# Joining the two products with the high weight into one 512-column matmul (second layer's gate/up)

## Chip, cores, metric

One core of one Trainium2 chip. The metric is the device time of one execution in microseconds, as the median of several runs. The kernel before takes 1451.1 us (three runs, 1447.51 to 1451.57).

## What is computed

Two transformer blocks on 256 tokens of width 1024, one after the other. The second one has two layers, and in its second layer only the 256 latent tokens go on (the context is no longer needed), so its SwiGLU works on 256 columns:

```python
def swiglu(h, w_gate_up, w_down):
    gu = h @ w_gate_up
    g, u = jnp.split(gu, 2, axis=-1)
    return (jax.nn.silu(g) * u) @ w_down
...
h = h + g_f * swiglu(modulate(rmsnorm_2(h, norm_ffn[i]), sh_f, sc_f), ffn_w_gate_up[i], ffn_w_down[i])
```

`w_gate_up` is 1024 x 5632 in float32 (2816 features of gate, as many of up). The stage that computes `gu` and `silu(g) * u` in the second layer is called `gu1` in the kernel; `dn1` is the product with `w_down` after it.

## The kernel before

**Numbers in two parts.** TensorE multiplies in fp32r. Weights and activations are each split into a high part (a cast) and a low part (the rest): x = xh + xl, w = wh + wl. A product is three matmuls into the same PSUM place: wh with xh, wh with xl, wl with xh (`three`, lines 1050 to 1054). The weights are the stationary operand, 128x128; the activations, features on partitions and tokens on columns, the moving one: 256 columns in `gu1`, 512 in the first layer's `gu0`.

**Weights.** They come from memory in units of 128x1024 (four k tiles by 256 features, 512 KB), into four slots. For each unit SyncE starts the transfer into `raw` (line 392), ScalarE casts `raw` to `wh` (`high`, line 637), GpSimd subtracts to make `wl` (`low`, line 547), and TensorE waits for that (`unit_ready`). ScalarE casts a unit only when TensorE is done with the unit four before it. A step is two units: all 8 k tiles for 256 features.

**The stage.** In gate/up the 256 features of a step are 128 of gate and the 128 of up that belong to them: a pair. There are 22 steps, unrolled by two in a loop; the first trip is written out. For one output tile (gate or up) TensorE runs over four k tiles of a unit, three matmuls each. Gate and up of 256 columns each share one bank: pair j of the two uses bank j (`tile_bank`, `pair_banks`). Pairs alternate, so TensorE fills one while the other is read.

After a pair is done, `gate_up` of ScalarE (line 859) and of VectorE (line 1668) work on it in turn: Silu of the gate half (line 867), product with the up half (line 1674, which frees the pair), the high part of f (ScalarE, line 870), its low part (VectorE, line 1677). The order on ScalarE is by hand. A trip for pair j is: the casts of the two units of the next step (`high_step`), then Silu and high part for pair j. So the casts for step j+2 stand behind Silu and high part of pair j.

**Around it.** Ahead of the stage the activations are normalized and split (lines 1488 to 1496 and 741); behind it comes `dn1`, for which `stream_summed` first loads another activation table (line 665) and then goes on with the casts. The names that the change adds are `xhl` (xh and xl in one tile), `sf` (a place in SBUF for the copied halves), `joined` and the semaphores `small_gu1` and `joined_gu1`.

Of the kernel before, what the change touches and what calls it, by code (L numbers as in the profile page):

```python
# [8 lines left out]
F32R = mybir.dt.float32r  # L9
BF16 = mybir.dt.bfloat16  # L10
ALU = mybir.AluOpType
ACT = mybir.ActivationFunctionType
AX_X = mybir.AxisListType.X

P = 128
D = 1024
KT = D // P
SEQ = 256
NT = 2 * SEQ
# [86 lines left out]
ADA_SLOTS = 4  # L106
ADA_WOVEN = {"out": (3, 3, 0, 6)}
OUT_ROWS = ((0, 1, 2), (3,), (4,), (5,))
IN_U = (0, 1, 4, 5, 2, 3, 6, 7)
_at = 6  # L110
for _n, _per, _slots in (("gu", 1, 2), ("dn", 3, 3), ("gu0", 2, 2), ("dn0", 3, 2)):
# [35 lines left out]
def build(nc, wall, wada, cond, xin, pin, par, tab, tab_ret, tab_rope, tab_mask, rpb, out):  # L147
    with ExitStack() as ctx:
        sems = {}

        def S(name):
            if name not in sems:
                sems[name] = ctx.enter_context(nc.semaphore(name))
            return sems[name]
# [8 lines left out]
        def at(name, shape, offset, dt=F32):  # L163
            size = 4 * int(np.prod(shape[1:]))
            assert offset + size <= base + arena_bytes, (name, offset + size - base - arena_bytes)
            return nc.alloc_sbuf_tensor_at(name, shape, dt, offset=offset)

        def sb(name, shape, dt=F32):
            o = cursor[0]
            cursor[0] = (o + 4 * int(np.prod(shape[1:])) + 31) // 32 * 32  # L170
            return at(name, shape, o, dt)

        class Region:
# [5 lines left out]
            def take(self, name, shape, dt=F32):  # L179
# [5 lines left out]

        h = sb("h", [P, KT, NT])
        xs_at = cursor[0]
        xh = sb("xh", [P, KT, NT], F32R)
        xl = sb("xl", [P, KT, NT], F32R)
        y = sb("y", [P, KT, NT])  # L190
        y_at = cursor[0] - 4 * KT * NT
        raw = sb("raw", [P, SLOTS, HALF, 256])
        wh = sb("wh", [P, SLOTS, HALF, 256], F32R)
        wl = sb("wl", [P, SLOTS, HALF, 256], F32R)
# [18 lines left out]
        fh = {SEQ: at("fh1", [P, FT, SEQ], big_at, F32R), NT: at("fh2", [P, FT, NT], big_at, F32R)}  # L213
        fl = {SEQ: at("fl1", [P, FT, SEQ], big_at + 4 * FT * SEQ, F32R),
              NT: at("fl2", [P, FT, NT], big_at + 4 * FT * NT, F32R)}
        sil = at("sil", [P, 2, NT], y_at)
        ft = at("ft", [P, 2, NT], y_at + 8 * NT)

# [57 lines left out]
        ps = ctx.enter_context(nc.psum_tensor("ps", [P, 8, 512], F32))  # L276
# [6 lines left out]
        bank_free = S("bank_free")  # L283
# [5 lines left out]
        def pair_banks(j, n, wide=False):  # L289

            if n == SEQ and wide:
                return ps[:, 2 * j:2 * j + 2, 0:SEQ]
            if n == SEQ:
                return ps[:, j, :].rearrange("p (a b) -> p a b", a=2)
            return ps[:, 2 * j:2 * j + 2, :]

        def tile_bank(j, o, n, wide=False):

            return ps[:, j, o * SEQ:o * SEQ + SEQ] if n == SEQ and not wide else ps[:, 2 * j + o, 0:n]
# [29 lines left out]
        def pair_done(eng, ph, i, pair):  # L329

            eng.wait_ge(units_done, i * (2 * ph.body) + (2 * ph.step0 + 2 * ph.per_pair * (pair + 1) + SLOTS))
# [57 lines left out]
        def _(sp):  # L389
# [86 lines left out]
            sp.dma_start(ident[:], tab).then_inc(S("tab_in"), 16)  # L476
            load(0, 0, IN_U[0])
            sp.dma_start(prm[:], par).then_inc(S("prm_in"), 16)
            for u_ in range(1, SLOTS):
                load(u_, u_, IN_U[u_])  # L480
            for u_ in range(SLOTS, SLOTS + 2):
                load(u_, u_ % SLOTS, IN_U[u_])
            sp.dma_start(csb[:], bass.AP(cond.tensor, 0, [[0, P], [D, 2], [1, D]])).then_inc(S("cond_in"), 16)
# [148 lines left out]
        def _(act):  # L632
# [226 lines left out]
            def gate_up(ph, n, f0):  # L859

                def body(i, ahead=0):
                    for j in range(2):
                        if j >= ahead:
                            high_step(ph, i, j)
                        pair_done(act, ph, i, j)
                        act.wait_ge(S("f_lo"), i * 2 + (f0 + j + 1))
                        nc.scalar.activation(sil[:, j, 0:n], tile_bank(j, 0, n), ACT.Silu).then_inc(S("silu_ready"), 1)  # L867
                        act.wait_ge(bank_free, i * 2 + (ph.pair0 + j + 3))
                        settled(act)
                        nc.scalar.activation(fh[n][:, i * 2 + j, :], ft[:, j, 0:n], ACT.Copy).then_inc(S("f_hi"), 1)  # L870
                if ph.name == "gu1":
                    second_step(ph)
                if ph.name != "gu0":
                    preload(ACT.Silu)
                body(0, 1)
                with act.Fori(1, ph.iters) as i:
                    body(i)
# [6 lines left out]
            ph = PH["pg"]  # L884
# [15 lines left out]
            for l in range(2):  # L900
# [124 lines left out]
                n = NT if l == 0 else SEQ  # L1025
# [14 lines left out]
        def _(pe):  # L1040
# [9 lines left out]
            def three(o, wa, wb, xa, xb, start, stop):  # L1050

                nc.tensor.matmul(o, wa, xa, start=start, stop=False, skip_group_check=True)  # L1052
                nc.tensor.matmul(o, wa, xb, start=False, stop=False, skip_group_check=True)  # L1053
                return nc.tensor.matmul(o, wb, xa, start=False, stop=stop, skip_group_check=True)  # L1054

            def features(ph, n, a=xh, b=xl, ktiles=KT, fresh=None, wide=False, within=None):


                def body(i):
                    for j in range(ph.body):  # L1060
                        pair = j // ph.per_pair
                        if j % ph.per_pair == 0:
                            banks_ready(ph, i, pair)
                        for half in range(2):
                            slot = unit_ready(ph, i, j, half)
                            k0 = 2 * HALF * (j % ph.per_pair) + HALF * half
                            for o in range(2):
                                c = slice(o * P, o * P + P)
                                if within and isinstance(i, int) and (i, j) == (0, 0) and (half, o) in within:
                                    within[half, o]()  # L1070
                                for kk in range(min(HALF, ktiles - k0)):
                                    k = k0 + kk
                                    if fresh and o == 0 and pair == 0:
                                        sem, n0, each = fresh
                                        pe.wait_ge(S(sem), n0 + each * (k + 1))
                                    mm = three(tile_bank(pair, o, n, wide), wh[:, slot, kk, c], wl[:, slot, kk, c],
                                               a[:, k, 0:n], b[:, k, 0:n], k == 0 and (n == NT or wide or o == 0), k == ktiles - 1)
                            mm.then_inc(units_done, 1)
                run(pe, ph, body, ph.iters - 1 if within else 0)
# [108 lines left out]
            for c in range(CONV_T):  # L1188
                mm = nc.tensor.matmul(ps[:, 2, 0:SEQ], ones[:], cy[:, c, :], start=c == 0, stop=c == CONV_T - 1)
# [13 lines left out]
            for hd in range(RET_H):  # L1203
                pe.wait_ge(S("ret_s"), hd + 1)
                c = slice(hd * P, hd * P + P)
                nc.tensor.matmul(ps[:, 6, c], st[:, hd, 0:P], vb[:, 0, c], start=True, stop=True)
                nc.tensor.matmul(ps[:, 7, c], st[:, hd, P:256], vb[:, 0, c], start=True, stop=False)
                mm = nc.tensor.matmul(ps[:, 7, c], st[:, hd, 256:384], vb[:, 1, c], start=False, stop=True)
            mm.then_inc(S("ret_o"), 1)
            pe.wait_ge(S("dev_sq"), 1)  # L1210
            for c in range(CONV_T):
                mm = nc.tensor.matmul(ps[:, 5, 0:SEQ], ones[:], sq[:, c, 0:SEQ], start=c == 0, stop=c == CONV_T - 1)
# [3 lines left out]
            for hd in range(RET_H):  # L1216
                for t in range(2):
                    mm = nc.tensor.transpose(ps[:, hd // 2, (hd % 2) * 256 + t * P:(hd % 2) * 256 + t * P + P],
                                             on[:, t, hd, :], ident[:])
# [35 lines left out]
            for l in range(2):  # L1255
                n = NT if l == 0 else SEQ
# [188 lines left out]
        def _(dve):  # L1445
            link = Link(dve, "dve_link")
            V = nc.vector
# [171 lines left out]
            def take_summed(ph, dst, norm):  # L1619

                for p in range(4):
                    if ph.name == "out":
                        condition(ph, 0, 0, OUT_ROWS[p])
                    else:
# [43 lines left out]
            def gate_up(ph, n, f0):  # L1668
                def body(i):
                    for j in range(2):  # L1670
                        condition(ph, i, j)
                        dve.wait_ge(S("f_lo"), i * 2 + (f0 + j + 1))
                        dve.wait_ge(S("silu_ready"), i * 2 + (f0 + j + 1))
                        V.tensor_tensor(ft[:, j, 0:n], sil[:, j, 0:n], tile_bank(j, 1, n), ALU.mult).then_inc(bank_free, 1)  # L1674
                        dve.wait_ge(S("f_hi"), i * 2 + (f0 + j + 1))
                        f1 = bass.ds(i * 2 + j, 1)
                        V.tensor_tensor(fl[n][:, f1, :].rearrange("p a b -> p (a b)"), ft[:, j, 0:n],  # L1677
                                        fh[n][:, f1, :].rearrange("p a b -> p (a b)").bitcast(F32),
                                        ALU.subtract).then_inc(S("f_lo"), 1)
                run(dve, ph, body)  # L1680
# [12 lines left out]
            ph = PH["in_u"]  # L1693
# [121 lines left out]
            for l in range(2):  # L1815
                n = NT if l == 0 else SEQ
# [292 lines left out]
```

## Time and profile before

| | |
|---|---|
| median of three runs | 1451.1 us |
| profiled execution | 1450.42 us, span 1448.6 us |
| granted TensorE clock, mean | 0.981 |
| TensorE busy | 1403.9 us (97%) |
| GpSimd busy | 841.1 us (58%) |
| VectorE busy | 710.3 us (49%) |
| ScalarE busy | 607.0 us (42%) |
| the stage `gu1` | from about 1247 to 1374.9 us |
| the stage `dn1` | 1374.9 us to about 1439 us |

Times in the trace are from the start of the span. The table's busy shares are over the whole span; the stage of the change is about 9% of it and has to be read by itself. Matmuls overlap one another, so that the duration of one (0.28 us for 256 columns) is not its cost; the distance from one start to the next is.

### The profile page before, as it was taken

How to read it: one execution, taken by the hardware profiler on the slowest of the kernel's cores; microseconds unless marked ns; L12 is line 12 of the kernel's file. 1: busy time of each engine (PE TensorE's matmuls, PEld its weight loads, DVE VectorE, ACT ScalarE, POOL GpSimd, SP SyncE). 2: the span in 40 equal slices, each digit the busy share in tenths (PEclk: the TensorE clock that was granted, in tenths of full speed). 3: DMA queues.
4: the chain of work that ended last, by engine and by line, in shares of the span. 5: the costliest groups of instructions: out<-in, count | busy, mean ns of one | idle time of the engine just before them, and what ended most of it. 6: DMA issues, size and time to landing. Idle time of an engine off the chain costs nothing.

```text
span 1448.6 us, 25731 instructions
## 1 busy us (share of the span) xinstructions
PE 1403.9 (97%) x9145; PEld 1256.8 (87%) x9145; DVE 710.3 (49%) x1324; ACT 607.0 (42%) x973; POOL 841.1 (58%) x420
## 2 busy tenths in 40 slices
PE   9998999999999999799999999999999999999998
PEld 8988999999888888687888888888888788999997
DVE  5977555555714555836655555333424383311111
ACT  5454554544524445634332332322331365444452
POOL 5836788797474676052444344544365443588895
PEclk9998999999999999899999999999999999999999
DMA  7836477785332222031656555554393102455563
GB/s 255 267 112 211 160 275 274 276 309 171 123 102 73 74 73 88 1 117 61 228 176 210 184 185 207 185 179 141 86 255 99 44 18 68 132 180 184 177 211 105
DMA packets 82987, 227.27 MB, mean 157 GB/s; under 512 B 23664, under 2 KB 29040, under 8 KB 82672
## 3 DMA queue, kind: packets, MB, share of 16 engines
q1 hardware_dynamic: 82480, 224.91, 46.7%
q10 hardware_dynamic: 448, 1.57, 0.5%
q8 instruction: 37, 0.61, 0.2%
q14 instruction: 22, 0.18, 0.0%
HBM read 222.26 MB, written 1.05 MB: 154 GB/s over the span
## 4 chain that ended last, share of the span: by engine, by line
issue 37%; PE 30%; POOL 27%; DVE 3%; ACT 2%; POOLq 1%; DMA 0%; ACTq 0%; DVEq 0%
POOL wl L547 25%; PE ps L1052 6%; PE ps L1054 6%; PE ps L1053 6%; PE ps L1139 1%; PE ps L1115 1%; PE ps L1116 1%; PE ps L1117 1%; PE ps L1386 1%; PE ps L1125 1%; POOL xl L567 1%; PE ps L1312 1%; PE ps L1333 1%; PE ps L1400 1%; PE ps L1378 1%
## 5 line engine op out<-in xcount | busy, mean ns | idle before, releaser
L547 POOL TENSOR_TENSOR wl<-raw,wh 128x1024 fp32r<-128x1024 f32 x310 | 743.3, 2418 | 542.4 <-ACT wh L637 542.0
L1052 PE MATMUL ps<-xh,wh 128*128 128x256 f32 (+1 forms) x1728 | 562.3, 325 | 10.7 <-DVE y L1629 4.3
L1053 PE MATMUL ps<-xl,wh 128*128 128x256 f32 (+1 forms) x1728 | 556.6, 322 | 0.0
L1054 PE MATMUL ps<-xh,wl 128*128 128x256 f32 (+1 forms) x1728 | 556.3, 322 | 0.0
L637 ACT ACTIVATE wh<-raw 128x1024 fp32r<-128x1024 f32 x310 | 318.7, 1053 | 285.8 <-PE ps L1054 205.0
L1052 PEld LDWEIGHTS ps<-xh,wh 128*128 128x128 f32 x1728 | 332.1, 192 | 43.0 <-issue 8.2
L1054 PEld LDWEIGHTS ps<-xh,wl 128*128 128x128 f32 x1728 | 331.8, 192 | 24.3
L1053 PEld LDWEIGHTS ps<-xl,wh 128*128 128x128 f32 x1728 | 332.0, 192 | 22.7
L1052 PE MATMUL ps<-fh,wh 128*128 128x256 f32 (+1 forms) x528 | 168.8, 320 | 1.7 <-POOL wl L547 1.7
L1053 PE MATMUL ps<-fl,wh 128*128 128x256 f32 (+1 forms) x528 | 168.6, 319 | 0.0
L1054 PE MATMUL ps<-fh,wl 128*128 128x256 f32 (+1 forms) x528 | 168.6, 319 | 0.0
L1674 DVE TENSOR_TENSOR ft<-sil,ps 128x256 f32<-128x256 f32 (+1 forms) x66 | 33.7, 510 | 190.2 <-ACT sil L867 190.2
L867 ACT ACTIVATE sil<-ps 128x256 f32<-128x256 f32 (+1 forms) x66 | 30.1, 455 | 213.9 <-PE ps L1054 213.9
L1052 PEld LDWEIGHTS ps<-fh,wh 128*128 128x128 f32 x528 | 99.3, 188 | 10.2 <-POOL wl L547 2.1
L1053 PEld LDWEIGHTS ps<-fl,wh 128*128 128x128 f32 x528 | 99.3, 188 | 8.1
L1054 PEld LDWEIGHTS ps<-fh,wl 128*128 128x128 f32 x528 | 99.3, 188 | 8.0
L1662 DVE SCALAR_TENSOR_TENSOR h<-ps,mod,h 128x256 f32<-128x256 f32 x48 | 20.3, 478 | 172.8 <-PE ps L1054 172.8
L1535 DVE SCALAR_TENSOR_TENSOR unread<-ada_late,ps 128x1024 bf16<-128x1024 f32 x56 | 68.3, 1219 | 13.8 <-DMA ada_late<-wada 7.7
L1538 DVE SCALAR_TENSOR_TENSOR unread<-ada_late,ps 128x1024 bf16<-128x1024 f32 x56 | 68.4, 1221 | 6.9 <-DVE unread L1535 1.7
L1677 DVE TENSOR_TENSOR fl<-ft,fh 128x256 f32 (+1 forms) x66 | 34.8, 527 | 51.2 <-ACT fh L870 51.2
L930 ACT ACTIVATE e<-ps,sm 128x512 f32<-128x512 f32 (+1 forms) x64 | 36.4, 577 | 54.7 <-DVE sm L1841 38.7
L870 ACT ACTIVATE fh<-ft 128x256 f32 (+3 forms) x66 | 32.3, 489 | 53.3 <-DVE ft L1674 53.3
(219 smaller groups left out, 1659.6 us busy)
## 6 DMA issues: line engine op xcount, KB each, us to landing
raw<-wall SPq DMA_DIRECT2D x310, 512.0 KB, 3.9
ada_late<-wada SPq DMA_DIRECT2D x56, 512.0 KB, 3.4
ada<-wada SPq DMA_DIRECT2D x40, 512.0 KB, 3.5
bias<-rpb SPq DMA_DIRECT2D x16, 256.0 KB, 6.1
sww<-qk SPq DMA_DIRECT2D x16, 128.0 KB, 2.3
h<-xin SPq DMA_DIRECT2D x1, 1024.0 KB, 6.4
csb<-cond SPq DMA_DIRECT2D x1, 1024.0 KB, 6.2
h<-xin SPq DMA_DIRECT2D x2, 512.0 KB, 5.2
```

The source lines that it names most:

```text
L547: nc.gpsimd.tensor_tensor(wl[:, slot, :, :], raw[:, slot, :, :], wh[:, slot, :, :].bitcast(F32), ALU.subtract).then_inc(lo_ready, 1)
L637: nc.scalar.activation(wh[:, slot, :, :], raw[:, slot, :, :], ACT.Copy).then_inc(hi_ready, 1)
L867: nc.scalar.activation(sil[:, j, 0:n], tile_bank(j, 0, n), ACT.Silu).then_inc(S("silu_ready"), 1)
L870: nc.scalar.activation(fh[n][:, i * 2 + j, :], ft[:, j, 0:n], ACT.Copy).then_inc(S("f_hi"), 1)
L930: nc.scalar.activation(e2[:, q, m, c], ps[:, b + m, c], ACT.Exp, scale=0.125, bias=sm[:, r6, 2 * t + m:2 * t + m + 1], accum_out=sm[:, r6, ...
L1052: nc.tensor.matmul(o, wa, xa, start=start, stop=False, skip_group_check=True)
L1053: nc.tensor.matmul(o, wa, xb, start=False, stop=False, skip_group_check=True)
L1054: return nc.tensor.matmul(o, wb, xa, start=False, stop=stop, skip_group_check=True)
L1535: V.scalar_tensor_tensor(junk, unit, 1.0, both[0], ALU.mult, ALU.mult, accum_out=mod_flat[:, at_, 0]).then_inc(S("ada_half"), 1)
L1538: ins = V.scalar_tensor_tensor(junk, unit, 1.0, both[1], ALU.mult, ALU.mult, accum_out=mod_flat[:, at_, 1])
L1674: V.tensor_tensor(ft[:, j, 0:n], sil[:, j, 0:n], tile_bank(j, 1, n), ALU.mult).then_inc(bank_free, 1)
L1677: V.tensor_tensor(fl[n][:, f1, :].rearrange("p a b -> p (a b)"), ft[:, j, 0:n], fh[n][:, f1, :].rearrange("p a b -> p (a b)").bitcast(F32) ...
```

## The change

In `gu1` alone, the products of wh with xh and with xl become one matmul with 512 moving columns (xh's 256 and, 16 KB further in the same tile, xl's 256), which writes a whole bank: the left half gets wh by xh, the right half wh by xl. The product of wl with xh is added to the right half. Gate and up now have a bank each, a pair has two. When a pair is done, ScalarE copies the right halves of both banks to SBUF (`sf`), VectorE adds them to the left halves in PSUM, and Silu and product read the left halves. The last matmul of a pair, the order of the weight casts and everything outside `gu1` stay.

```diff
--- before.py
+++ after.py
@@ -106,6 +106,7 @@
 ADA_SLOTS = 4
 ADA_WOVEN = {"out": (3, 3, 0, 6)}
 OUT_ROWS = ((0, 1, 2), (3,), (4,), (5,))
+JOINED = ('gu1',)
 IN_U = (0, 1, 4, 5, 2, 3, 6, 7)
 _at = 6
 for _n, _per, _slots in (("gu", 1, 2), ("dn", 3, 3), ("gu0", 2, 2), ("dn0", 3, 2)):
@@ -185,8 +186,8 @@
 
         h = sb("h", [P, KT, NT])
         xs_at = cursor[0]
-        xh = sb("xh", [P, KT, NT], F32R)
-        xl = sb("xl", [P, KT, NT], F32R)
+        xhl = sb("xhl", [P, 2, KT, NT], F32R)
+        xh, xl = xhl[:, 0, :, :], xhl[:, 1, :, :]
         y = sb("y", [P, KT, NT])
         y_at = cursor[0] - 4 * KT * NT
         raw = sb("raw", [P, SLOTS, HALF, 256])
@@ -213,6 +214,7 @@
         fh = {SEQ: at("fh1", [P, FT, SEQ], big_at, F32R), NT: at("fh2", [P, FT, NT], big_at, F32R)}
         fl = {SEQ: at("fl1", [P, FT, SEQ], big_at + 4 * FT * SEQ, F32R),
               NT: at("fl2", [P, FT, NT], big_at + 4 * FT * NT, F32R)}
+        sf = at("sf", [P, 2, 2, NT], y_at)
         sil = at("sil", [P, 2, NT], y_at)
         ft = at("ft", [P, 2, NT], y_at + 8 * NT)
 
@@ -864,7 +866,12 @@
                             high_step(ph, i, j)
                         pair_done(act, ph, i, j)
                         act.wait_ge(S("f_lo"), i * 2 + (f0 + j + 1))
-                        nc.scalar.activation(sil[:, j, 0:n], tile_bank(j, 0, n), ACT.Silu).then_inc(S("silu_ready"), 1)
+                        if ph.name in JOINED:
+                            nc.scalar.activation(sf[:, :, j, SEQ:NT], ps[:, 2 * j:2 * j + 2, SEQ:NT], ACT.Copy)\
+                                .then_inc(S(f"small_{ph.name}"), 1)
+                            act.wait_ge(S(f"joined_{ph.name}"), i * 2 + (j + 1))
+                        nc.scalar.activation(sil[:, j, 0:n], tile_bank(j, 0, n, ph.name in JOINED), ACT.Silu)\
+                            .then_inc(S("silu_ready"), 1)
                         act.wait_ge(bank_free, i * 2 + (ph.pair0 + j + 3))
                         settled(act)
                         nc.scalar.activation(fh[n][:, i * 2 + j, :], ft[:, j, 0:n], ACT.Copy).then_inc(S("f_hi"), 1)
@@ -1053,6 +1060,12 @@
                 nc.tensor.matmul(o, wa, xb, start=False, stop=False, skip_group_check=True)
                 return nc.tensor.matmul(o, wb, xa, start=False, stop=stop, skip_group_check=True)
 
+            def joined(o, wa, wb, k):
+
+                nc.tensor.matmul(o, wa, xhl[:, :, k, 0:SEQ], start=k == 0, stop=False, skip_group_check=True)
+                return nc.tensor.matmul(o[:, SEQ:2 * SEQ], wb, xh[:, k, 0:SEQ], start=False, stop=k == KT - 1,
+                                        skip_group_check=True)
+
             def features(ph, n, a=xh, b=xl, ktiles=KT, fresh=None, wide=False, within=None):
 
 
@@ -1073,6 +1086,9 @@
                                     if fresh and o == 0 and pair == 0:
                                         sem, n0, each = fresh
                                         pe.wait_ge(S(sem), n0 + each * (k + 1))
+                                    if ph.name in JOINED:
+                                        mm = joined(ps[:, 2 * pair + o, :], wh[:, slot, kk, c], wl[:, slot, kk, c], k)
+                                        continue
                                     mm = three(tile_bank(pair, o, n, wide), wh[:, slot, kk, c], wl[:, slot, kk, c],
                                                a[:, k, 0:n], b[:, k, 0:n], k == 0 and (n == NT or wide or o == 0), k == ktiles - 1)
                             mm.then_inc(units_done, 1)
@@ -1670,8 +1686,13 @@
                     for j in range(2):
                         condition(ph, i, j)
                         dve.wait_ge(S("f_lo"), i * 2 + (f0 + j + 1))
+                        if ph.name in JOINED:
+                            dve.wait_ge(S(f"small_{ph.name}"), i * 2 + (j + 1))
+                            V.tensor_tensor(pair_banks(j, n, True), pair_banks(j, n, True), sf[:, :, j, SEQ:NT], ALU.add)\
+                                .then_inc(S(f"joined_{ph.name}"), 1)
                         dve.wait_ge(S("silu_ready"), i * 2 + (f0 + j + 1))
-                        V.tensor_tensor(ft[:, j, 0:n], sil[:, j, 0:n], tile_bank(j, 1, n), ALU.mult).then_inc(bank_free, 1)
+                        V.tensor_tensor(ft[:, j, 0:n], sil[:, j, 0:n], tile_bank(j, 1, n, ph.name in JOINED), ALU.mult)\
+                            .then_inc(bank_free, 1)
                         dve.wait_ge(S("f_hi"), i * 2 + (f0 + j + 1))
                         f1 = bass.ds(i * 2 + j, 1)
                         V.tensor_tensor(fl[n][:, f1, :].rearrange("p a b -> p (a b)"), ft[:, j, 0:n],
```

## Rows read from the trace of the kernel before

**Rows 1.** The page, busy tenths in 40 slices, and the granted clock

```profile
PE   9998999999999999799999999999999999999998
...
PEclk9998999999999999899999999999999999999999
```

**Rows 2.** Groups by line and shape, 1252 to 1375 us: busy, mean ns | idle before, releaser

```profile
L547 POOL TENSOR_TENSOR wl<-raw,wh 128x1024 fp32r<-128x1024 f32 x44 | 104.9, 2406 | 33.1 <-ACT wh L637 33.1
```

**Rows 3.** Waits, 1252 to 1375 us: who waited for whom, total us, times, longest

```profile
POOL wl L547 <- ACT wh L637: 33.1, 21, 12.7
...
PE ps L1052 <- POOL wl L547: 0.2, 1, 0.2
```

**Rows 4.** Timeline, first matmuls of two steps: start, duration, engine, line, operation

```profile
1305.79 0.28 PE L1052 MATMUL ps<-xh,wh 128*128 128x256 f32 x1
...
1311.55 0.28 PE L1052 MATMUL ps<-xh,wh 128*128 128x256 f32 x1
```

**Rows 5.** Timeline, TensorE in the first layer's gate/up, twelve intervals apart

```profile
739.68 0.39 PE L1052 MATMUL ps<-xh,wh 128*128 128x512 f32 x1
...
742.40 0.39 PE L1052 MATMUL ps<-xh,wh 128*128 128x512 f32 x1
```

**Rows 6.** Timeline, the other engines after the step that ends at 1305.79

```profile
1306.07 0.38 ACT L867 ACTIVATE sil<-ps 128x256 f32<-128x256 f32 x1 [2.40 <-PE ps L1054]
...
1306.56 0.42 DVE L1674 TENSOR_TENSOR ft<-sil,ps 128x256 f32<-128x256 f32 x1 [4.21 <-ACT sil L867]
...
1307.12 0.42 ACT L870 ACTIVATE fh<-ft 128x256 f32 x1 [0.67 <-DVE ft L1674]
...
1307.53 2.01 ACT L637 ACTIVATE wh<-raw 128x1024 fp32r<-128x1024 f32 x2
...
1308.67 4.76 POOL L547 TENSOR_TENSOR wl<-raw,wh 128x1024 fp32r<-128x1024 f32 x2 [1.10 <-ACT wh L637]
...
1314.32 4.77 POOL L547 TENSOR_TENSOR wl<-raw,wh 128x1024 fp32r<-128x1024 f32 x2 [0.89 <-ACT wh L637]
```

**Rows 7.** Timeline, by engine, from the stage into the down stage

```profile
1374.91 0.28 PE L1052 MATMUL ps<-fh,wh 128*128 128x256 f32 x1
...
1376.68 1.28 ACT L665 ACT_TABLE_LOAD   x1
...
1378.08 3.88 ACT L637 ACTIVATE wh<-raw 128x1024 fp32r<-128x1024 f32 x4
...
1379.20 37.66 POOL L547 TENSOR_TENSOR wl<-raw,wh 128x1024 fp32r<-128x1024 f32 x16 [2.53 <-ACT wh L637]
...
1380.49 0.28 PE L1054 MATMUL ps<-fh,wl 128*128 128x256 f32 x1
1381.63 0.39 PE L1052 MATMUL ps<-fh,wh 128*128 128x256 f32 x1 [0.86 <-POOL wl L547]
```

**Rows 8.** Groups by line and shape, whole span: operations like the added ones

```profile
L1000 ACT ACTIVATE pt<-ps 128x512 f32<-128x512 f32 x32 | 17.4, 595 | 22.0 <-PE ps L1386 18.7 <-PE ps L1378 3.3
...
L1674 DVE TENSOR_TENSOR ft<-sil,ps 128x512 f32<-128x512 f32 x22 | 15.1, 688 | 62.3 <-ACT sil L867 62.3
...
L1950 DVE TENSOR_TENSOR ps<-ps,bias 128x512 f32<-128x512 f32 x16 | 11.2, 698 | 18.3 <-PE ps L1400 18.3
```

**Rows 9.** Timeline, VectorE to ScalarE in the unrolled first trip

```profile
1254.16 0.42 DVE L1674 TENSOR_TENSOR ft<-sil,ps 128x256 f32<-128x256 f32 x1 [3.14 <-ACT sil L867]
...
1254.61 0.42 ACT L870 ACTIVATE fh<-ft 128x256 fp32r<-128x256 f32 x1 [0.56 <-DVE ft L1674]
```

**Rows 10.** Timeline, TensorE and ScalarE at the stage's start

```profile
1253.85 0.39 PE L1052 MATMUL ps<-xh,wh 128*128 128x256 f32 x1 [0.22 <-POOL wl L547]
...
1259.91 0.38 ACT L867 ACTIVATE sil<-ps 128x256 f32<-128x256 f32 x1 [2.98 <-PE ps L1054]
```

**Rows 11.** Stretches: length, busy PE, PEld, DVE, ACT, POOL, granted clock, DMA share, GB/s

```profile
1200.00:1250.00 50.00, 46.35 (x360) 43.69 (x357) 18.22 (x45) 24.54 (x43) 19.00 (x8) 0.93 0.26 85
...
1300.00:1350.00 50.00, 50.00 (x419) 50.00 (x418) 7.63 (x18) 24.72 (x36) 41.13 (x18) 1.00 0.57 183
```

## Prediction

> **What bounds the kernel now.** I read the forty slices of the page first: TensorE is busy 0.9 or more in all but three of them, and its granted clock is at 0.9 or more in all but two [rows 1]. A change to the second layer's gate/up stage (about 1247 to 1375 us) can therefore pay only by making TensorE's own stream shorter there, and it loses as soon as TensorE waits for something new. So the second question is who comes close behind TensorE in that stage. In the groups of the stretch 1252 to 1375 us it is GpSimd, which makes the low halves of the weights (line 547): 104.9 of the 123 us [rows 2]. The waits of the same stretch say what starts it: it waits 33.1 us for ScalarE's casts (line 637), and TensorE waits for GpSimd only 0.2 us, once [rows 3]. The supply of weights is on time; what must be found is by how much. That is no busy share, it is read off one step in the timeline.
>
> One step is one weight step of 8 k tiles: two units, 48 matmuls, one pair (gate and up of 128 features). The stretch from 1305.79 to 1311.55 is one step: 5.76 us, a matmul each 120 ns [rows 4]. The granted clock there is 1.00, the 2.4 GHz level [rows 11], at which 256 columns take 106.7 ns: 13.3 ns of each start-to-start are not columns. In the first layer's gate/up of the second block (512 columns) the twelve intervals from 739.68 to 742.40 take 2.72 us, 226.7 ns each: 213.3 of columns and again 13.3 [rows 5].
>
> The supply is a loop through four engines [rows 6]. Take the step that ends, by the first matmul of the next, at 1305.79. ScalarE's Silu begins at 1306.07, VectorE's product at 1306.56, ScalarE's high half of f at 1307.12, and only then, in ScalarE's own order (`high_step` of the next trip stands behind it), the two casts of weights at 1307.53. GpSimd starts the first low half at 1308.67 and needs 2.40 (its mean in rows 2 is 2.41). These are weights of the step after next, which starts at 1311.55. The other parity of the two-step loop is the same, with GpSimd at 1314.32 after a boundary at 1311.55. TensorE starts 0.03 us after a low half ends (1379.20 + 2.40, and TensorE at 1381.63) [rows 7]. So from the end of a step to the first weights of the step after next the loop takes 1308.67 + 2.43 - 1305.79 = 5.31 us and 1314.32 + 2.43 - 1311.55 = 5.20 us; mean 5.26. TensorE needs them after 5.76. **The cover is 0.5 us.** On that number the case turns.
>
> **What the change takes off TensorE.** Each k tile's three matmuls of 256 columns become one of 512 and one of 256: 360 ns become 226.7 + 120 = 346.7. A step has 16 such triples: 5.76 - 16 x 0.0133 = 5.55 us. Over 22 steps that is 4.7 us if nothing else moves. The columns stay; only a start-up per triple goes. No row shows a moving operand in two pieces (xh and xl of one tile, 16 KB apart). From below I take 226.7, the row of the same shape; from above 240, where joining gives nothing back.
>
> Of the overhead per matmul the Trainium skill (TensorE: Matmul & The Clock Gate, "Wait — 56ns, not 53.3ns?") says that warm matmuls start every N / 2.4 GHz plus about 2.5 ns. The rows at both sizes disagree, with 13.3 ns. By that page joining would save an estimated 16 x 2.5 ns = 0.04 us a step, 0.9 us in the stage where the rows give 4.7, and the sum below would come to 1462.5.
>
> **What it adds, and where.** Each step gets, inside the loop just read and ahead of the casts: ScalarE copies the two right halves to SBUF (128x512 out of PSUM), VectorE adds them in place (PSUM and SBUF to PSUM, 128x512), and only then Silu may start. ScalarE's plain copy of 128x512 from PSUM is line 1000: 0.595. VectorE's add of exactly this form, two banks in place, is line 1950: 0.698; the product of line 1674 at 128x512 is 0.688 [rows 8]. Two hand-overs come with them. ScalarE to VectorE takes 0.11 (Silu ends 1306.45, product starts 1306.56). VectorE to ScalarE takes 0.14 in the loop (1306.98 to 1307.12) [rows 6], but 0.03 in the unrolled first trip (1254.16 + 0.42 to 1254.61) [rows 9]; the Silu behind the new add has constant addresses but a wait on a register, so I take 0.09. Sum: 0.60 + 0.11 + 0.70 + 0.09 = **1.50 us** a step; between 1.40 (a copy of 0.58, 0.10, 0.69, 0.03) and 1.56 (0.60, 0.12, 0.70, 0.14). What waits behind it: on ScalarE the Silu, the cast of f and both weight casts; on GpSimd both low halves; on TensorE the step after next. The banks (free 2.7 us after the step's end instead of 1.2) are needed again only 5.5 us after it. VectorE, busy 7.6 of 50 us [rows 11], has room for 22 adds; the new semaphore counts I take at nothing.
>
> **The sum.** The loop becomes 5.26 + 1.50 = 6.76 us, against a TensorE step of 5.55: the cover is gone and TensorE waits. With each wait comes a refill: the first matmul after the wait at 1381.63 lasts 0.39 where the others last 0.28, so 0.11 more [rows 7]. The casts behind step j gate step j+2, so two steps take 6.76 + 0.11 + 5.55 = 12.42 us. Now they take 11.53: the Silu of step 1 begins at 1259.91 [rows 10], 0.28 after the step's end as at 1306.07, so that ended at 1259.63; the first matmul of the down stage is at 1374.91 [rows 7]; 115.28 us for 20 steps. The second unit of a step doesn't wait: its low half ends 2.4 after the first's, and TensorE takes 2.8 for the first. The 20 steps that hang on the loop cost 10 x 0.89 = +8.9 us.
>
> Start of the stage: step 1 already waits for its low half and starts at 1253.85 [rows 10], behind a ScalarE that splits the stage's inputs. The change moves that not at all, so step 0 saves nothing. Step 1 now ends at 1253.85 + 0.11 + 5.55 = 1259.51: -0.1 us.
>
> End of the stage: here the trace holds an experiment of its own. Behind the last pair ScalarE loads a table and runs a dummy activation, so that its casts begin at 1378.08, not at 1376.68: the loop is 1.40 longer. TensorE, due 0.12 after 1380.49, starts at 1381.63, 1.02 late [rows 7]: 1.40 less a cover of 0.4. The new work adds the whole of its 1.50 to that wait: +1.5. After it GpSimd makes 16 low halves in 37.66 us, 2.35 each, for units of 2.85 of TensorE's: nothing waits further, and nothing is recovered.
>
> Total +8.9 - 0.1 + 1.5 = **+10.3 us**. The profiled execution took 1450.4 (span 1448.6), 0.7 under the median of 1451.1; 1450.4 + 10.3 = **1460.7 us**. The bounds 1.40 and 1.56 enter 11 times: 1459.6 to 1461.4. With the spread of the runs before (1447.51 to 1451.57) this case's own range is 1457 to 1463.
>
> **The rivals.** (a) *The loop keeps its cover and the matmuls' gain comes through: faster.* With d for the added work, waits appear above d = 5.55 - 5.26 = 0.29 us, and the whole is zero where 10 x (10.92 + d - 11.53) + d - 0.1 = 0, d = 0.56 us. Below 0.29 the change gains at most the 4.7 less step 0's 0.2 and the d at the stage's end: 1446 to 1447. For it speaks only that the stage has no waits now. Against it: the copy alone takes 0.6, and the table load shows that 1.4 us in this very place reaches TensorE. Chance 0.05. (b) *Joining gives nothing back* (the long matmul takes 240): the step stays 5.76 and two take 12.63: 11.0 + 1.5 = 12.5, 1462.9. For it: no row has such an operand. Against it: 13.3 ns at both sizes. Chance 0.1; the page named above would put the time close to this. (c) *TensorE's clock falls, because it idles some 0.66 us in each 6.2.* For it: the stretch 1200 to 1250, where TensorE was busy 46.35 of 50, had 0.93 [rows 11]; the stage would be at 5.55 of 6.21, 0.89. Against it: the last slice of the page has TensorE in the eighths and the clock still at 0.9 or more [rows 1]. At 0.93 a step takes 5.97, two steps 0.42 more: +4.2, 1464.9. Chance 0.05. (d) *The added work overlaps with something, so that d is near 0.8, half of what the rows give*: 11 x 0.8 - 6.2 = +2.6, 1453. Nothing in the code lets the copy, the add and the Silu overlap. Chance 0.05. The forecast keeps 0.75.
>
> **How the numbers follow.** The likeliest case gives 1460.7. To hold 8 in 10 the range takes that case's own range and (b) and (c) with their spread: 1456.5 to 1465.5, and leaves (a) and (d) out. A measurement of this kernel tells about 0.3%, 4.4 us, from no change: slower means above 1455.5, which is the forecast, (b) and (c), 0.90. Within 0.3%: (d) with 0.05 and 0.03 of (a), which at its best reaches just that bound: 0.08. Faster by over 0.3%: the other 0.02 of (a).
>
> **What would show it in the changed kernel's profile.** Matmul starts in the stage 227 and 120 ns apart in turn. ScalarE's order in a step: copy, Silu, cast of f, two weight casts, which begin some 3.2 us after the step's end instead of 1.7. VectorE's add near 0.70. TensorE waiting for line 547 for 0.5 to 0.7 us in nearly every step from step 2 on, or twice as long in every second, some 13 us in all; steps of 6.2 us; 2.5 us of wait at the second step of the down stage; granted clock 1.00. The prediction is wrong if TensorE shows no waits in the stage, if a 512-column start-to-start is over 240 ns, or if the weight casts don't come later by the sum of the two new operations.

## The result

The changed kernel takes 1459.1 us (median of four runs, 1457.9 to 1460.6); the kernel before, in runs on the same chips, 1449.7 (1447.5 to 1451.6). The ratio is 1.0067, 95% interval 1.0053 to 1.0082: slower by 9.4 us. (The ratios given here and below are those on record; they differ from the quotients of the medians by up to 0.12%, and no conclusion hangs on which of the two is taken.) The prediction was +10.3 us, 1460.7 (1456.5 to 1465.5). The profiled execution of the changed kernel has a span of 1456.6 us, 8.0 more than that of before.

The page of the changed kernel: TensorE's line, its busy tenths and its granted clock answer to [rows 1]; the first line has the busy time of every engine.

```profile
PE 1405.0 (96%) x8793; PEld 1237.7 (85%) x8793; DVE 725.1 (50%) x1346; ACT 620.8 (43%) x995; POOL 840.7 (58%) x420
...
PE   9999999999999998799999999999999999999998
...
PEclk9989999999999999999999999999999999999999
```

352 matmuls fewer (8793 where 9145 were), and a share of 96 where it was 97%: fewer start-ups, and more waiting. By slices nothing can be seen; the stage has to be opened. Groups of its stretch 1252 to 1383 us, by line and shape (busy, mean ns, then idle before and its releaser), which answer to [rows 2] and [rows 8]:

```profile
L1065 PE MATMUL ps<-xhl,wh 128*128 128x512 f32 x335 | 120.1, 402 | 6.8 <-POOL wl L549 6.6
L549 POOL TENSOR_TENSOR wl<-raw,wh 128x1024 fp32r<-128x1024 f32 x43 | 102.1, 2396 | 28.9 <-ACT wh L639 28.9
...
L1691 DVE TENSOR_TENSOR ps<-ps,sf 128x512 f32<-128x512 f32 x22 | 15.4, 700 | 76.2 <-ACT sf L870 76.2
L870 ACT ACTIVATE sf<-ps 128x512 f32<-128x512 f32 x21 | 12.6, 599 | 30.9 <-PE ps L1066 30.9
```

Copy and add cost what the rows of like operations gave (0.599 and 0.700; 0.595 and 0.698 in [rows 8]). TensorE's 0.2 us of waiting for the low halves [rows 3] has become 7.0 in the stage, and its 0.9 at the end [rows 7] has become 2.1. The waits of the stretch 1247 to 1395 us (total, times, longest):

```profile
PE ps L1065 <- POOL wl L549: 7.0, 12, 0.9
...
PE ps L1059 <- POOL wl L549: 2.1, 1, 2.1
```

One trip of the loop in the timeline, read as [rows 6]. The step that ends just before it (its copy begins 0.28 after the next step's first matmul, as Silu did) ends at 1318.75 - 0.28 = 1318.47:

```profile
1318.75 0.60 ACT L870 ACTIVATE sf<-ps 128x512 f32<-128x512 f32 x1 [1.93 <-PE ps L1066]
...
1319.38 0.70 DVE L1691 TENSOR_TENSOR ps<-ps,sf 128x512 f32<-128x512 f32 x1 [3.88 <-ACT sf L870]
...
1320.11 0.38 ACT L873 ACTIVATE sil<-ps 128x256 f32<-128x256 f32 x1 [0.77 <-DVE ps L1691]
...
1320.53 0.42 DVE L1694 TENSOR_TENSOR ft<-sil,ps 128x256 f32<-128x256 f32 x1 [0.45 <-ACT sil L873]
...
1321.08 0.42 ACT L877 ACTIVATE fh<-ft 128x256 f32 x1 [0.58 <-DVE ft L1694]
...
1321.50 2.01 ACT L639 ACTIVATE wh<-raw 128x1024 fp32r<-128x1024 f32 x2
...
1322.63 4.75 POOL L549 TENSOR_TENSOR wl<-raw,wh 128x1024 fp32r<-128x1024 f32 x2 [1.93 <-ACT wh L639]
```

And TensorE's waits in the timeline: every second step from 1300 us on (before that, in every step up to 1293.96, up to 0.7 us late each time), and the long one in the down stage, which answers to the end of [rows 7]:

```profile
1300.46 0.50 PE L1065 MATMUL ps<-xhl,wh 128*128 128x512 f32 x1 [0.68 <-POOL wl L549]
...
1312.71 0.51 PE L1065 MATMUL ps<-xhl,wh 128*128 128x512 f32 x1 [0.67 <-POOL wl L549]
...
1325.08 0.50 PE L1065 MATMUL ps<-xhl,wh 128*128 128x512 f32 x1 [0.86 <-POOL wl L549]
...
1388.15 0.58 PE L1059 MATMUL ps<-fh,wh 128*128 128x256 f32 x1 [2.12 <-POOL wl L549]
```

From the copy's start to the first cast it is 1321.50 - 1318.75 = 2.75 us, where from Silu's start it was 1.46 [rows 6]. The loop from the step's end to the weights is 1325.08 - 1318.47 = 6.61 us where it was 5.31, and two steps take 1325.08 - 1312.71 = 12.37 us where they took 11.53.

The 8.0 us between the two spans come together as follows. The two ends of the stage, by TensorE's matmuls:

```profile
1251.30 0.50 PE L1065 MATMUL ps<-xhl,wh 128*128 128x512 f32 x1 [0.37 <-POOL wl L549]
...
1380.17 0.28 PE L1059 MATMUL ps<-fh,wh 128*128 128x256 f32 x1
```

From the start of step 1 (after its first wait, 1251.30 here, 1253.85 in [rows 10]) to the first matmul of the down stage (1380.17; 1374.91 in [rows 7]) it is 128.87 instead of 121.06: **+7.8**. From there to the first matmul behind the wait, 1388.15 - 1380.17 = 7.98 instead of 6.72: **+1.3**. From there to the end of the span, 1456.6 - 1388.15 = 68.45 instead of 66.97: **+1.5**. The stage began 2.55 us earlier, of which the code of the change is no cause that I can see: 1.6 of them are there already at the first block's gate/up (first Silu at 160.41, 162.03 before). That part moves from execution to execution; the runs of before alone spread over 4 us. The three parts that the change touches give +10.6, the medians +9.4.

### The profile page after: what moved, and what is told of

Read it like the earlier page. It is cut to its first block, busy times and chain, and to the rows that moved or that the text cites. A ratio compares the mean times of both kernels' runs of the same rounds, so it can differ in the third digit from the quotient of the medians.

```text
span 1456.6 us, 25091 instructions
## 1 busy us (share of the span) xinstructions
PE 1405.0 (96%) x8793; PEld 1237.7 (85%) x8793; DVE 725.1 (50%) x1346; ACT 620.8 (43%) x995; POOL 840.7 (58%) x420
## 4 chain that ended last, share of the span: by engine, by line
issue 37%; PE 28%; POOL 26%; DVE 2%; ACT 1%; POOLq 1%; DVEq 0%; ACTq 0%
POOL wl L549 24%; PE ps L1059 6%; PE ps L1060 6%; PE ps L1061 6%; PE ps L1131 1%; PE ps L1132 1%; PE ps L1133 1%; PE ps L1402 1%; PE ps L1155 1%; POOL xhl L569 1%; PE ps L1328 1%; PE ps L1141 1%; PE ps L1349 1%; PE ps L1416 1%; PE ps L1394 1%
## 5 line engine op out<-in xcount | busy, mean ns | idle before, releaser
L1059 PE MATMUL ps<-xhl,wh 128*128 128x256 f32 (+1 forms) x1376 | 461.0, 335 | 7.4 <-POOL wl L549 2.4
L1060 PE MATMUL ps<-xhl,wh 128*128 128x256 f32 (+1 forms) x1376 | 455.7, 331 | 0.0
L1061 PE MATMUL ps<-xhl,wl 128*128 128x256 f32 (+1 forms) x1376 | 455.4, 331 | 0.0
L1059 PEld LDWEIGHTS ps<-xhl,wh 128*128 128x128 f32 x1376 | 263.4, 191 | 39.6 <-POOL wl L549 4.5
L1061 PEld LDWEIGHTS ps<-xhl,wl 128*128 128x128 f32 x1376 | 263.1, 191 | 23.9
L1060 PEld LDWEIGHTS ps<-xhl,wh 128*128 128x128 f32 x1376 | 263.3, 191 | 22.6
L1065 PE MATMUL ps<-xhl,wh 128*128 128x512 f32 x352 | 126.7, 403 | 8.0 <-POOL wl L549 7.0
L1066 PE MATMUL ps<-xhl,wl 128*128 128x256 f32 x352 | 98.6, 280 | 0.0
L1065 PEld LDWEIGHTS ps<-xhl,wh 128*128 128x128 f32 x352 | 66.1, 188 | 29.4 <-POOL wl L549 12.1
```

The costliest lines, as they stand in the source:

```text
L1065: nc.tensor.matmul(o, wa, xhl[:, :, k, 0:SEQ], start=k == 0, stop=False, skip_group_check=True)
L1066: return nc.tensor.matmul(o[:, SEQ:2 * SEQ], wb, xh[:, k, 0:SEQ], start=False, stop=k == KT - 1, skip_group_check=True)
```

## The experiments

The theory: what is lost is the cover of a loop through ScalarE, VectorE and GpSimd, from a pair's end to the weights of the step after next, into which the copy and the add were put. The first rival: the 512-column matmul itself (operand in two pieces, wide banks) costs the time.

**The casts taken out of the loop, with and without joining.** In the changed kernel:

```diff
                         pair_done(act, ph, i, j)
...
                             nc.scalar.activation(sf[:, :, j, SEQ:NT], ps[:, 2 * j:2 * j + 2, SEQ:NT], ACT.Copy)\
                                 .then_inc(S(f"small_{ph.name}"), 1)
+                            high_step(ph, i, j + 1)
                             act.wait_ge(S(f"joined_{ph.name}"), i * 2 + (j + 1))
```

with the `high_step` ahead of `pair_done`, and that of the down stage's first trip, left out, since their casts are now made.

> The changed kernel with one thing moved on ScalarE in this stage: the two weight casts for the step after next stand right behind the copy, ahead of Silu, and the same for the last pair, whose casts are the down stage's second step (so the table load is behind them too). Nothing else is altered. Theory (the loop from a pair's end to the weights of the step after next lost its cover): the loop falls to 0.28 + 0.60 + 1.05 + 0.12 + 2.40 + 0.03 = 4.5 us against a TensorE step of some 5.6; no wait for the low half in the stage, none of 1 to 2.4 us in the down stage; the joined matmuls' gain comes through, 22 x 0.17 = 3.7 us, plus the 1.0 us of the wait that the kernel before has in its down stage: 4 to 5 us under the kernel before, ratio near 0.997. Rival (the 512-column matmul with its two-piece operand, or the wide banks, cost the time): no gain, 8 to 10 us over the kernel before as in the changed kernel.

Measured: 1444.7 us against 1449.7 of before, ratio 0.9977 (0.9966 to 0.9987). It is faster than both kernels, with the same joined matmuls, the same copy and the same add. A trip in its timeline:

```profile
1307.49 0.60 ACT L872 ACTIVATE sf<-ps 128x512 f32<-128x512 f32 x1 [1.78 <-PE ps L1069]
1307.99 1.99 ACT L639 ACTIVATE wh<-raw 128x1024 fp32r<-128x1024 f32 x2
1309.88 0.37 ACT L876 ACTIVATE sil<-ps 128x256 f32<-128x256 f32 x1
...
1309.12 4.98 POOL L549 TENSOR_TENSOR wl<-raw,wh 128x1024 fp32r<-128x1024 f32 x2 [0.56 <-ACT wh L639]
```

The casts stand 0.50 behind the copy's start, GpSimd starts 1.91 after the step's end (1307.49 - 0.28 = 1307.21) instead of 4.16 (1322.63 - 1318.47), and TensorE waits for a low half once in the stage, at its second step, as before. From there to the down stage it takes 116.59 us:

```profile
1251.63 0.50 PE L1068 MATMUL ps<-xhl,wh 128*128 128x512 f32 x1 [0.38 <-POOL wl L549]
...
1368.22 0.28 PE L1062 MATMUL ps<-fh,wh 128*128 128x256 f32 x1
```

The wait in the down stage is gone too. So the long matmul isn't what costs; the loop is.

> The kernel before with the same move: weight casts for the step after next at the head of ScalarE's work on a pair, ahead of Silu. Matmuls as before. It says how much of e1 is the move and not the joining. Theory: the stage is as it was, 5.76 us a step, for it had 0.5 us of cover already; only the wait of 1.0 us at the down stage's second step goes: 1 us under the kernel before, ratio 0.9993. Rival (the casts' place limits the stage already in the kernel before): over 3 us under it.

Measured: ratio 0.9997 (0.9989 to 1.0006), 1448.3 us. The stage is as it was: 121.06 us from step 1 to the down stage, exactly that of before, and the wait of 1.0 us in the down stage is gone. So the move alone is worth about a microsecond (1.1 by the traces, all of it in the down stage; the interval allows 1.6), and the rest of e1's gain needs the joined matmuls. VectorE shows a side of the move, told below.

**The added work alone.** In the kernel before, with its three matmuls of 256 columns:

```diff
+                        if ph.name == "gu1":
+                            nc.scalar.activation(sf[:, :, j, SEQ:NT], pair_banks(j, n), ACT.Copy, scale=0.0)\
+                                .then_inc(S("small_gu1"), 1)
+                            act.wait_ge(S("joined_gu1"), i * 2 + (j + 1))
                         nc.scalar.activation(sil[:, j, 0:n], tile_bank(j, 0, n), ACT.Silu).then_inc(S("silu_ready"), 1)
...
+                            V.tensor_tensor(pair_banks(j, n), pair_banks(j, n), sf[:, :, j, SEQ:NT], ALU.add)\
+                                .then_inc(S("joined_gu1"), 1)
```

> The kernel before with the added work alone: ScalarE copies both halves of the pair's bank (128x512) scaled by zero to the same place in SBUF, VectorE adds them in place in PSUM, and Silu waits for that, in the stage of the change only; matmuls are the three of 256 columns. Theory: two steps take 5.31 + 1.30 + 0.11 + 5.76 = 12.48 us instead of 11.53, +9.5, and 1.3 at the down stage with 1.5 of slow matmuls behind that wait: about 12 us over the kernel before, more than the changed kernel, since no matmul is saved. Rival (the long matmul is what costs): the time of the kernel before.

Measured: 1462.9 us, ratio 1.0103 (1.0087 to 1.0118), 13 us over the kernel before by the medians (15 by the ratio) and more than the changed kernel. The traces of the two kernels give the 12 that was expected: 130.22 us from step 1 to the down stage instead of 121.06, and 76.54 from there to the end instead of 73.69. In the later half of the stage TensorE waits in every second step again, and two steps take 12.47 us (1364.64 to 1377.10 is 12.46), as worked out:

```profile
1252.74 0.39 PE L1057 MATMUL ps<-xh,wh 128*128 128x256 f32 x1 [0.21 <-POOL wl L548]
...
1364.64 0.39 PE L1057 MATMUL ps<-xh,wh 128*128 128x256 f32 x1 [0.69 <-POOL wl L548]
...
1377.10 0.39 PE L1057 MATMUL ps<-xh,wh 128*128 128x256 f32 x1 [0.69 <-POOL wl L548]
...
1382.96 0.28 PE L1057 MATMUL ps<-fh,wh 128*128 128x256 f32 x1
```

Between this kernel and the changed one lies the joining. In a stage that waits it is worth 1.35 us (130.22 against 128.87), since only the steps that don't wait get shorter. The medians are 3.8 us apart; of the rest the two traces have only 0.1 behind the stage (76.54 against 76.43) and 1.4 ahead of it, where executions differ anyway.

**The joined matmuls alone** (copy and add taken out of both engines):

> The changed kernel without copy and add: the joined matmuls run into the wide banks, but Silu and product read the left halves alone, so the product of the high weight with the low part of the activations and that of the low weight with the high part, which stand in the right halves, are left out of the result in this stage. Theory: a loop of 5.3 us against a step of 5.6: no waits in the stage, the matmuls' gain alone, 3 to 4 us under the kernel before, ratio near 0.9975, and the same 1.0 us wait in the down stage. Rival (the long matmul costs): as slow as the changed kernel or at best equal to the kernel before.

Measured: 1445.9 us, ratio 0.9976 (0.9966 to 0.9987). No waits in the stage after its second step, 118.81 us from step 1 to the down stage instead of 121.06, and the wait of 1.1 us in the down stage as before. The rival is out from this side too.

```profile
1252.26 0.50 PE L1061 MATMUL ps<-xhl,wh 128*128 128x512 f32 x1 [0.37 <-POOL wl L549]
...
1371.07 0.28 PE L1055 MATMUL ps<-fh,wh 128*128 128x256 f32 x1
```

**How the cost grows with the added work.** The copy without the add, and the copy twice:

```diff
-                            act.wait_ge(S(f"joined_{ph.name}"), i * 2 + (j + 1))
...
-                            V.tensor_tensor(pair_banks(j, n, True), pair_banks(j, n, True), sf[:, :, j, SEQ:NT], ALU.add)\
-                                .then_inc(S(f"joined_{ph.name}"), 1)
```

> The changed kernel with the copy but without the add (the products in the right halves are left out of the result in this stage). The added work on the loop is ScalarE's copy alone, 0.60 to 0.63 us. Theory (loop): 5.31 + 0.62 = 5.93 us from a pair's end to the weights, against a step of 5.6: small waits in every second step, two steps 11.6 to 11.7 us where the kernel before has 11.53: 0.7 to 1.7 us over twenty steps, and 0.6 at the down stage, so 1 to 2 us over the kernel before, ratio 1.0005 to 1.0015, near the zero crossing of 0.56 us that the prediction worked out. Rival (the cost is mainly in the add, in PSUM, or in the hand-overs): the time of the joined matmuls alone, 4 us under the kernel before.

Measured: 1448.7 us, ratio 0.9994 (0.9984 to 1.0005): neither what the theory nor what the rival gave, and not to be told from the kernel before. The timeline says why it came out under the theory's figure:

```profile
1340.62 0.60 ACT L870 ACTIVATE sf<-ps 128x512 f32<-128x512 f32 x1 [1.98 <-PE ps L1065]
1341.12 0.38 ACT L872 ACTIVATE sil<-ps 128x256 f32<-128x256 f32 x1
...
1341.60 0.42 DVE L1689 TENSOR_TENSOR ft<-sil,ps 128x256 f32<-128x256 f32 x1 [4.27 <-ACT sil L872]
```

Silu starts 0.50 after the copy's start, not 0.62: with no engine between them, the second begins before the first's 0.60 is over. The stage takes 120.78 us, 0.3 less than before, and TensorE waits 0.5 us longer in the down stage: +0.2 by the traces.

```diff
+                            nc.scalar.activation(sf[:, :, j, SEQ:NT], ps[:, 2 * j:2 * j + 2, SEQ:NT], ACT.Copy)\
+                                .then_inc(S("twice"), 1)
+                            act.wait_ge(S("twice"), i * 2 + (j + 1))
                             nc.scalar.activation(sf[:, :, j, SEQ:NT], ps[:, 2 * j:2 * j + 2, SEQ:NT], ACT.Copy)\
                                 .then_inc(S(f"small_{ph.name}"), 1)
```

> The changed kernel with the copy done twice, one after the other: 0.60 to 0.66 us more on the loop. Theory: the cost is linear in the added work, eleven times it: two steps 12.97 instead of 12.37, +6.0, and +0.6 at the down stage: 6.6 to 7.3 us over the changed kernel, about 16.5 us over the kernel before, ratio 1.0115. Rival (ScalarE's time is hidden and the add or something else limits): under 2 us over the changed kernel.

Measured: 1467.0 us, ratio 1.0109 (1.0096 to 1.0122), where 1.0115 was expected. The second copy starts 0.63 after the first:

```profile
1339.46 0.60 ACT L870 ACTIVATE sf<-ps 128x512 f32<-128x512 f32 x1 [1.35 <-PE ps L1069]
1340.09 0.60 ACT L873 ACTIVATE sf<-ps 128x512 f32<-128x512 f32 x1
```

With the four points, all with joined matmuls, the line can be drawn; d is the work added to the loop by the timelines, the stage is counted from step 1 to the down stage:

| | d, us | stage, us | ratio to before |
|---|---|---|---|
| kernel before | 0 | 121.06 | 1 |
| joined alone (e4) | 0 | 118.81 | 0.9976 |
| copy (e5) | 0.50 | 120.78 | 0.9994 |
| copy and add (the change) | 1.30 | 128.87 | 1.0067 |
| copy twice and add (e7) | 1.93 | 135.27 | 1.0109 |

From 0.50 to 1.93 the stage grows by 10.1 us for each microsecond of d, as ten double steps must. Drawn on downwards, this line meets e4's 118.81 at d = 0.30, where the prediction has the first waits above 0.29; no run lies between 0 and 0.50. The prediction's zero crossing, 0.56, counts the down stage too: there e5 gives +0.2 at 0.50, so that it lies just below 0.5.

**The end of the stage by itself.** The changed kernel, with e1's move for the last pair only:

> The changed kernel with the two weight casts moved ahead of add and Silu for the last pair of the stage alone, so that the down stage's second step has its weights early and the table load stands behind the casts; the other 21 pairs as in the changed kernel. Theory (the end is a term of its own): TensorE's wait of 2.4 us there goes, and with it the stretch at the lower clock level that followed it in the changed kernel (0.80 to 0.86 from 1385 to 1395 us): 2.3 + 1.5 = 3.8 us under the changed kernel, about 5.6 us over the kernel before, ratio 1.004; the waits of every second step stay. Rival (the lower clock behind the wait costs nothing in the median, or has another cause): 2.3 us under the changed kernel, ratio 1.005, or the lower clock stays.

Measured: 1456.1 us, ratio 1.0040 (1.0028 to 1.0053), 1.004 as expected; the waits in the stage stay (128.60 us), the one in the down stage is gone. From the down stage's first matmul to the end of the span it takes 72.57 us instead of the changed kernel's 76.43: 3.9 us less (as the ratios have it, 0.0027 of 1449.7; the medians have 3.0), for 2.3 us of wait. Most of the rest is TensorE's clock. Stretches of the changed kernel and, below, of this one (length, busy of TensorE, its weight loads, VectorE, ScalarE and GpSimd, then the granted clock, DMA share, GB/s):

```profile
1385.00:1390.00 5.00, 2.88 (x17) 2.68 (x16) 0.00 (x0) 3.50 (x4) 4.26 (x2) 0.80 0.17 47
1390.00:1395.00 5.00, 5.00 (x39) 5.00 (x38) 0.00 (x0) 1.06 (x1) 5.00 (x3) 0.86 0.68 230
```

```profile
1385.00:1390.00 5.00, 5.00 (x44) 5.00 (x43) 1.00 (x2) 3.80 (x5) 5.00 (x3) 1.00 0.66 214
1390.00:1395.00 5.00, 5.00 (x45) 5.00 (x44) 0.00 (x0) 2.12 (x2) 5.00 (x3) 1.00 0.68 220
```

Behind the wait the changed kernel's matmuls start 0.21 us apart instead of 0.12 (1388.74, 1388.95), which is the 1.2 GHz level.

**What stayed odd.** In e1 a joined pair of matmuls (512 and 256 columns) took 0.3467 us, as predicted, through the whole stage; in e4 0.3533 through the whole stage.

> The kernel of e1 once more, for one look at the distance of its matmul starts. In e1 a 512 and a 256 column matmul together took 0.3467 us through the whole stage, in e4 (the same matmuls) 0.3533 through the whole stage. If the distance belongs to the kernel's timing, it is 0.3467 again; if to the single execution, either may come. The prediction had 0.3467 from the rows of the two sizes; the difference is 16 x 0.0067 = 0.11 us a step, 2.3 us in the stage. No wait for the low half in the stage after its second step, as in e1.

> The kernel of e4 once more, for one look at the same distance: 0.3533 again if it belongs to the kernel's timing, either if it belongs to the execution. The products in the right halves are left out of the result, as in e4.

The kernel of e1 came out at 0.3533 this time, that of e4 at 0.3533 again (single runs of 1446.1 and 1449.4 us beside one of before of 1446.8). So the distance doesn't belong to the kernel: of the four executions without waits in the stage one had 0.3467 and three 0.3533. In the changed kernel it changes within one execution, from step to step: 0.3533 in 16 of the 21 steps from step 1 on, 0.3467 in five, of which four stand behind a wait. What sets it stays open; it is worth 0.11 us a step.

> The changed kernel once more, for one look at TensorE's clock behind the wait of 2.4 us at the down stage's second step: in its first profile the clock fell there (0.80 and 0.86 in the two stretches of 5 us), in e3 too, in e7 behind a wait of 2.6 us it didn't. If the fall hangs on the execution, it may be absent here; if on the kernel, it is there again.

The clock fell again (0.79 and 0.87 in the same two stretches; 1458.2 us). With e3 (0.69 in its stretch 1390 to 1395) that is three falls behind a wait across which two matmuls start 2.4 us apart, and one such distance of 2.6 us, in e7, with 1.00 before and after. A fall is thus likely there and not certain.

## Why the prediction was right, step by step

- **The cover of 0.5 us and the loop that uses it up**: right, and the point on which it all hung. e1 takes the casts out of the loop and gains, e3 puts the work in without the joining and loses 13 us, and the cost follows d at ten for one.
- **The added work, 1.50 us**: too large; measured 1.30, below its own lower bound of 1.40. Copy and add were right to 0.01; the hand-overs were too dear. From the copy's end to the add it is 0.03 (1318.75 + 0.60 to 1319.38), where 0.11 was taken from Silu to product, and from the add's end to Silu again 0.03, where 0.09 was taken. Besides, Silu to product shrank from 0.49 to 0.42 us. The same two engines thus hand over in 0.03 or in 0.11 and 0.14, depending on the instructions; with rows of other instructions the size was wrong by 0.2 us in all.
- **TensorE's step, 5.55 us**: 5.55 in e1 (116.59 over 21 steps), 5.65 in e4, e8 and e9 and in most steps of the changed kernel. Of the 13.3 ns a triple gives back 13.3 or 6.7, so that rival (b), which has nothing given back, is half true in most steps.
- **What joining gives back by the other figure**: by the 2.5 ns of the Trainium skill (TensorE: Matmul & The Clock Gate, "Wait — 56ns, not 53.3ns?"), set beside the rows in the prediction, the gain is an estimated 0.04 us a step. The runs show 0.11 to 0.21, so the rows were the better guide, though in three of the four executions without waits only half of what they gave came.
- **Two steps 12.42, twenty steps +8.9 less 0.1**: 12.37 and +7.8. The errors of d and of the step are opposite (0.2 less, 0.1 more), so that two steps come out almost right. The nine double steps from 1263.37 to 1374.42 take 12.34 each, 0.7 us less in all than predicted; the first and the last of the twenty steps take 6.12 and 5.75, together 0.6 less than a double step of 12.42; and step 1, also at 5.65 and with the next step 0.2 late, takes 0.3 more.
- **The waits' form**: both of those that were named, one after the other. Steps 2 to 8 each start late, by 0.1 to 0.7 us; from 1300 us on it is every second step, by 0.8 to 1.0. By matmul starts it is about 9 us in all instead of 13. The loop of either parity can run behind, and two waits of 0.4 or one of 0.9 give nearly the same double step (12.27 us from 1257.25 to 1269.52, 12.37 from 1325.08 to 1337.45).
- **The stage's end, +1.5**: +1.3 of wait, and e6 shows it as a term of its own. The 1.5 us behind it, most of it from slow matmuls, were missing from the sum: the prediction has nothing lost after the wait. Rival (c) had the lower clock in the wrong place: not in the stage, where TensorE idles 1 us in 12.4 and the clock stays at 1.00, but behind the one long wait.
- **Start of the stage**: step 1 waits as before (0.37 us, 0.22 before); right.
- The missing 1.5 and the surplus of 1.2 us in the other terms (8.8 for 7.8 in the stage, 1.5 for 1.3 at its end) nearly cancel, and the executions differ by 2.5 us ahead of the stage; that the total came within 1 us of the medians' difference is partly luck. So is that two steps came within 0.05 us, from two errors of opposite sign. The sign and the size of 10 us are not: e5, e7 and e3 lie on the same sum.

## What to carry to other kernels

Before work is added behind TensorE, find the loop by which it feeds TensorE's next input, and read its cover from one step of the timeline; here 0.5 us of cover stood against 1.3 us of added work, and the busy shares of ScalarE and VectorE, a half and a sixth in the stage, said nothing of it. Where an engine both drains one step and feeds another, put the feeding first: with the casts ahead of Silu the same change gains 0.23% where it lost 0.67%. And a wait at a seam costs more than its length when TensorE's clock falls behind it.

## What the runs showed of the hardware that was not expected

A copy and a Silu that follow each other on ScalarE overlap: in e5 0.50 us from start to start for a first operation of 0.60.

In e2 VectorE's last step, the low part of f (all operands in SBUF), takes 2.5 us on average instead of 0.47 in the same stretch before. The move of the casts has put GpSimd's low halves at the same time. Groups of the stretch 1252 to 1368 us in e2, and one case from its timeline:

```profile
L1679 DVE TENSOR_TENSOR fl<-ft,fh 128x256 f32 x20 | 50.2, 2508 | 14.1 <-ACT fh L872 14.1
```

```profile
1305.70 4.76 POOL L547 TENSOR_TENSOR wl<-raw,wh 128x1024 fp32r<-128x1024 f32 x2 [1.00 <-ACT wh L637]
...
1308.10 2.65 DVE L1679 TENSOR_TENSOR fl<-ft,fh 128x256 f32 x1 [0.73 <-ACT fh L872]
```

It ends at 1310.75, just behind GpSimd's second operation (1310.46). VectorE's product, which reads one operand from PSUM, keeps its 0.42 beside GpSimd (1306.95, inside GpSimd's first operation). The Trainium skill (Trainium Architecture — The Big Picture, "What this means for kernel authors") describes the port that the two share as "an exclusive lock (not a bandwidth split)"; the rows agree: VectorE's operation ends 0.29 us after GpSimd's, and GpSimd's keep their 4.76. Here it cost nothing, since nobody waits for the low part until the next pair; in e1 the operation comes at the change between GpSimd's two (at 1311.41, with the first from 1309.12 to 1311.53), keeps its 0.47 on average, and it is GpSimd's two that take longer, 4.98 us where they took 4.76.
